# Mask as eight extra contraction rows of the scores, scales moved to the queries, a negated maximum, and an earlier copy of finished values

## The reference

```python
# differential attention, 8 heads x 2 halves of 64
q = rope(q.reshape(B, S, H, 2, d), positions) * (d ** -0.5)
k = rope(k.reshape(B, S, H, 2, d), positions)
allowed = k_chunk[None, :] <= q_chunk[:, None]
s = jnp.where(allowed[None, None, None], einsum('bqhcd,bkhcd->bhcqk', qb, k), -jnp.inf)
p = jax.nn.softmax(s, axis=-1)
a = p[:, :, 0] - lam * p[:, :, 1]
# latent attention, 8 heads, 64 + 32 rows of contraction
sc = (einsum('bqhd,bkhd->bhqk', qn, k_nope) + einsum('bqhd,bkd->bhqk', qp, k_pe)) * scale   # 96 ** -0.5
sc = jnp.where(key_chunk[None, :] <= q_chunk[:, None], sc, -jnp.inf)
p = jax.nn.softmax(sc, axis=-1)
```

## Time and profile before

| what | us |
|---|---|
| median of 3 runs | 3967.03 (3963.65 to 3971.49) |
| the profiled execution, its own time | 3965.26 |
| its span, first to last instruction | 3963.4 |
| what lies around the span | 1.9 |
| differential attention, steps | 119 to 632 |
| latent attention, both layers, first scores to last values | 2947.8 to 3119, 3670.3 to 3844 |

### The profile page before, as it was taken

One profiled execution on the slowest core, in us unless ns is written; L12 is line 12 of the kernel. 1 busy time (PEld: TensorE's weight loads), 2 busy tenths in 40 slices (PEclk: granted clock), 3 DMA queues, 4 the chain that ended last, 5 costly groups with the idle time before them and its releaser, 6 DMA issues. The chain is left out here.

```text
span 3963.4 us, 44407 instructions
## 1 busy us (share of the span) xinstructions
PE 3634.3 (92%) x17688; PEld 2817.6 (71%) x17688; DVE 1662.8 (42%) x2161; ACT 1092.5 (28%) x1653; POOL 1142.8 (29%) x672
## 2 busy tenths in 40 slices
PE   6999987999999999999999998599969969996997
PEld 4777765888888888788888887487626758763565
DVE  5566755311121259641111123456536431363553
ACT  2344443101010116421001011215325310442540
POOL 3344512333333336433333332222201122230111
PEclk8999998999999999999999999799979979998898
DMA  3333322111111121211111110221042121203311
GB/s 122 106 124 131 107 85 80 48 48 48 48 48 48 64 74 54 85 46 48 49 48 48 48 48 21 91 94 53 9 133 54 59 96 43 75 22 90 86 60 59
DMA packets 80128, 267.22 MB, mean 67 GB/s; under 512 B 9424, under 2 KB 10608, under 8 KB 79984
## 3 DMA queue, kind: packets, MB, share of 16 engines
q1 hardware_dynamic: 54464, 191.30, 14.7%
q10 hardware_dynamic: 18608, 48.78, 3.6%
q0 software_dynamic: 6912, 25.17, 1.9%
HBM read 214.62 MB, written 46.40 MB: 66 GB/s over the span
## 5 line engine op out<-in xcount | busy, mean ns | idle before, releaser
L694 POOL CAST tk_w_hi<-tk_w_raw 128x1024 fp32r<-128x1024 f32 x160 | 178.1, 1113 | 1199.4 <-PE tk_acc L191 550.8
L191 PE MATMUL tk_acc<-tk_b_hi,tk_w_hi 128*128 128x512 f32 x1280 | 397.6, 392 | 11.4 <-POOL tk_w_lo L696 11.4
L191 PE MATMUL tk_acc<-tk_a_hi,tk_w_hi 128*128 128x512 f32 x1280 | 398.6, 393 | 3.5 <-POOL tk_w_lo L696 2.7
L191 PE MATMUL tk_acc<-tk_b_lo,tk_w_hi 128*128 128x512 f32 x1280 | 398.2, 392 | 0.0
L191 PE MATMUL tk_acc<-tk_b_hi,tk_w_lo 128*128 128x512 f32 x1280 | 398.1, 392 | 0.0
L191 PE MATMUL tk_acc<-tk_a_lo,tk_w_hi 128*128 128x512 f32 x1280 | 397.9, 392 | 0.0
L696 POOL TENSOR_TENSOR tk_w_lo<-tk_w_raw,tk_w_hi 128x1024 fp32r<-128x1024 f32 x160 | 394.1, 2463 | 12.8
L191 PE MATMUL tk_acc<-tk_a_hi,tk_w_lo 128*128 128x512 f32 x1280 | 397.6, 392 | 0.0
L841 ACT ACTIVATE tk_sq<-tk_r 128x1024 f32<-128x1024 f32 x64 | 67.9, 1061 | 1078.8 <-DVE tk_r L961 1078.8
L936 DVE TENSOR_TENSOR xT<-tk_acc,xT 128x1024 f32<-128x1024 f32 x80 | 98.0, 1225 | 614.9 <-PE tk_acc L191 614.9
L191 PEld LDWEIGHTS tk_acc<-tk_b_hi,tk_w_hi 128*128 128x128 f32 x1280 | 241.0, 188 | 65.0 <-POOL tk_w_lo L696 11.8
(11 more groups left out here) (363 smaller groups left out, 6748.6 us busy)
## 6 DMA issues: line engine op xcount, KB each, us to landing
tk_w_raw<-in_w_trunk SPq DMA_DIRECT2D x160, 512.0 KB, 3.2
da_w_mod<-in_ada_w POOLq DMA_DIRECT2D x48, 512.0 KB, 3.7
pj_w_raw<-in_w_in SPq DMA_DIRECT2D x44, 512.0 KB, 3.3
da_w_raw<-in_w_qkv SPq DMA_DIRECT2D x24, 512.0 KB, 3.7
x_dram<-xT ACTq DMA_DIRECT2D x24, 512.0 KB, 5.9
qk_dram<-xT ACTq DMA_DIRECT2D x32, 256.0 KB
ma_w_raw<-in_w_out SPq DMA_DIRECT2D x16, 512.0 KB, 4.1
xT<-x_dram SPq DMA_DIRECT2D x16, 512.0 KB, 7.9
```

The source lines that it names most:

```text
L191: last = pe.matmul(self.acc[:, u, s * HALF:(s + 1) * HALF], w[:, u, k, :], h[:, k, s * HALF:(s + 1) * HALF], start=(k == order[0] and part ...
L694: pool.tensor_copy(pn.hi[:, u, :, :], pn.raw[:, u, :, :]).then_inc(sems[f"w_hi{u}"], 1)
```

## The change

Four edits.

1. In `ma` the mask becomes part of the score matmuls. Rows 96 to 103 of q and k, one for each block of 128 tokens, are cleared by GpSimd (two memsets of 8 x 4096), then VectorE writes, with eight products of the identity, -1e30 into row 96 + b of q for the first 64 columns of block b, and 1 into row 96 + b of k for the last 64 columns of block b. The scores contract over 104 rows; the mask matmul is gone. TensorE waits for the eight products in place of three small memsets.
2. In `ma` and `da` VectorE's maximum is written with its sign turned, and the product with -scale is gone; the exponential has scale 1.
3. So queries carry the scale: in `mp` ScalarE's copy becomes an activation Copy with a scale; in `da` the four rotation products of queries and keys become `scalar_tensor_tensor` with the scale (or 1) as a third factor.
4. In `da` VectorE's `natural(t - 1)` moves from behind the maxima and rotations to the head of step t. The mask matmul of `da` stays.

```diff
@@ mla_project, ScalarE
-                        act.copy(ab[:, 0, at, :] if at < 2 else o[:, at % 2, :], acc[:, at % 2, :])\
-                            .then_inc(sems["out"], 1)
+                        act.activation(ab[:, 0, at, :] if at < 2 else o[:, at % 2, :], acc[:, at % 2, :], ACT.Copy,
+                                       scale=96 ** -0.5 if order[at] < 6 else 1.0).then_inc(sems["out"], 1)
@@ mixed_back
-        units, kd, scale = 4, 96, 96 ** -0.5
+        units, kd, rows, scale = 4, 96, 96 + SB, 96 ** -0.5
-                    pool.memset(mask[:, :, :], 0.0).then_inc(sems["mask"], 1)
-                    pool.wait_ge(sems["mask"], 1)
-                    pool.memset(mask[:, 0, 0:64], 1.0).then_inc(sems["mask"], 1)
-                    pool.memset(mask[:, 1, 64:128], NEG).then_inc(sems["mask"], 1)
+                    for x in (q, k):
+                        pool.memset(x[kd:rows, :, :, :], 0.0).then_inc(sems["clear"], 1)
-                    pe.wait_ge(sems["mask"], 3)
+                    pe.wait_ge(sems["mask"], 8)
-                            pe.matmul(dst[:, part, :], q[0:kd, u % 2, m, b * P:(b + 1) * P],
-                                      k[0:kd, u % 2, m, part * w:(part + 1) * w], start=True, stop=True)
-
-                        pe.matmul(dst[:, parts - 1, w - P:w], mask[:, 0, :], mask[:, 1, :], start=False,
-                                  stop=True, skip_group_check=True).then_inc(sems["scores"], 1)
+                            last = pe.matmul(dst[:, part, :], q[0:rows, u % 2, m, b * P:(b + 1) * P],
+                                             k[0:rows, u % 2, m, part * w:(part + 1) * w], start=True, stop=True)
+                        last.then_inc(sems["scores"], 1)
-                        dve.tensor_reduce(st[:, t % 4, 0, m:m + 1], score(m, parts, w), axis=AXXY, op=ALU.max)\
-                            .then_inc(sems["max"], 1)
-                        dve.wait_ge(sems["max"], i + 1)
-                        dve.tensor_scalar(st[:, t % 4, 1, m:m + 1], st[:, t % 4, 0, m:m + 1], -scale, None, ALU.mult)\
-                            .then_inc(sems["neg"], 1)
+                        dve.tensor_reduce(st[:, t % 4, 1, m:m + 1], score(m, parts, w), axis=AXXY, op=ALU.max,
+                                          negate=True).then_inc(sems["neg"], 1)
+                    for x, first, value in ((q, 0, NEG), (k, 64, 1.0)):
+                        dve.wait_ge(sems["clear"], 1 if x is q else 2)
+                        for u in range(2):
+                            for m in range(2):
+                                dst = x[kd:rows, u, m, :].rearrange("p (b n) -> p b n", b=SB)[:, :, first:first + 64]
+                                eye = self.ident[kd:rows, kd:rows].rearrange("p (b n) -> p b n", n=1)
+                                dve.tensor_scalar(dst, eye.broadcast_to([SB, SB, 64]), value, None, ALU.mult)\
+                                    .then_inc(sems["mask"], 1)
@@ attention_layer, VectorE (the maximum changes as above)
-                            dve.tensor_tensor(t4[:, 0, :], x, cos, ALU.mult)
+                            dve.scalar_tensor_tensor(t4[:, 0, :], x, by, cos, ALU.mult, ALU.mult)
...
                     for t in range(-1, nb + 4):
+                        natural(t - 1)
                         maximum(t + 1, 0)
                         maximum(t + 1, 1)
                         hp, due = pieces(t) if t >= 0 else (0, [])
                         for p in due:
                             rope(hp, p)
-                        natural(t - 1)
                         combine(t + 1)
```

More of the change, by code:

```diff
@@ L1756, in mixed_back @@
         names = PANEL_SEMS + [
-            "landed0", "landed1", "scores", "max", "neg", "exp", "prob", "pt", "pts", "pv", "out", "link", "mask",
+            "landed0", "landed1", "scores", "neg", "exp", "prob", "pt", "pts", "pv", "out", "link", "clear", "mask",
             "z_in0", "z_in1", "gated", "o_hi", "o_lo", "s_hi", "s_lo", "x_sq", "acc"] + [f"x_ld{n}" for n in range(DK)]
@@ L1768, in mixed_back @@
             st = sb("st", [P, 4, 4, 2])
-            mask = sb("mask", [1, 2, P], BF16)
             sc = ps("sc", [P, 2, S])
@@ L2043, in attention_layer @@
             "w_landed0", "w_landed1", "w_hi0", "w_hi1", "w_split0", "w_split1", "fa", "fb", "fv", "xa", "xb", "v_taken", "rot",
-            "stored", "table", "loaded", "dot", "lam", "landed0", "landed1", "scores", "neg", "max", "exp", "prob", "pt", "pts",
+            "stored", "table", "loaded", "dot", "lam", "landed0", "landed1", "scores", "neg", "exp", "prob", "pt", "pts",
             "pv", "nat", "ot", "out", "o_st0", "o_st1", "o_ld", "link", "mask", "nat_sq", "nat_sum", "nat_root", "nat_normed",
@@ L2382, in maximum @@
                         dve.wait_ge(sems["scores"], 2 * t + m + 1)
[L2383 to L2387 removed]
+                        dve.tensor_reduce(st[:, t % 4, 1, m:m + 1], sc[:, m, 0:parts, 0:w], axis=AXXY, op=ALU.max,
+                                          negate=True).then_inc(sems["neg"], 1)
                     def combine(t):
```

16 lines of the change are left out of this document (6 added, 10 removed).

## The result

In its first comparison the changed kernel took 3922.14 us (median of 4 runs, 3919.32 to 3925.07) and the kernel before 3969.26 (3963.65 to 3971.75): a ratio of 0.9885, 95% interval 0.9873 to 0.9897. A later comparison gave 0.9891 (0.9874 to 0.9908), 3927.49 against 3967.67. The forecast was 3941 us with a range from 3924 to 3957. The direction was right, the size was not: 45 us between the two profiled spans (3963.4 and 3918.5), where the sum said 25.8.

A forecast was written before the change was run, and what follows sets the result against it. TensorE was taken to bound `ma`, while in `da` it waits mostly for VectorE. 19.0 - 4.8 + 7.5 + 4.5 - 0.4 = 25.8 us off the profiled 3965.3, with 1.8 us added for the median: 3941 us, range 3924 to 3957.

The forecast's parts named there:

- Mask matmuls, 19.0 us: In `ma`, removing each mask matmul frees 0.25 us of TensorE in 38 of 64 halves: 9.5 us a layer.
- 26 of 64: Halves of an `ma` layer where TensorE already waits for ScalarE's copy, so removing the mask was to gain nothing.
- about +1 us: In `ma`, added gain from dearer masks at half clock at a layer's head and from the chained last steps.
- Rival (c): More comes back: a third of `da`'s low-clock stretches rise to 2.4 GHz, 4 us, waits 5 more; 3932 us, chance 0.2.
- Preparation, -4.8 us: At the head of each `ma` layer, the mask's memsets and products finish late, by 1.8 and 3.0 us.
- the held case: VectorE's first four mask products are held until GpSimd's second memset ends; mask ready at 12 us.
- nothing lost: Favourable bound for preparing the mask before `ma`'s first scores: no time lost; the other bound was 25.5 us in all.
- 104 rows at no cost: In `ma`, scores contracting over 104 rows in place of 96 keep the same pace by column, priced at nothing.
- Negated maximum, 4.5 us in `da`, nothing in `ma`: VectorE's shorter chain and earlier probabilities give 4.5 us in `da`, between 0 and 8; TensorE's queue hides it in `ma`.
- Moved copy, 7.5 us: In `da`, of 20.0 us of TensorE waits for VectorE's copy, 7.5 return as `prob` or exponentials take over; bounds 2 and 20.
- Scales, -0.4: ScalarE's scaled activation takes 0.1 us more than a copy, ten a layer; 0.2 us a layer shows.

The follow-up runs named there:

- w1_mask_steps_0_1: Changed kernel with the one-row mask matmul put back in the first two steps of each latent layer only; 3934.52 us, ratio 0.9911.
- w3_changed_again: The changed kernel run once more, unaltered, as the control of its batch; 3927.49 us, ratio 0.9891.
- y1_mask_first_unit: Changed kernel with the one-row mask matmul put back in the first of four units of each latent layer only; 3939.98 us, ratio 0.9929.
- y3_no_mask: Kernel before without mask matmuls in `ma` and without mask rows in their place, scores over 96 rows; 3940.31 us, ratio 0.9929.

## Why the prediction was wrong in size

- **Mask matmuls, 19.0 us: over-counted, in the right place.** At 2.4 GHz a unit gained 1.65 us, 6.7 a layer, 13.4 in all. The 0.25 us holds where transposes follow and is 0.16 where values do, and more halves than 26 of 64 run into ScalarE's copies: ten halves at 0.25 us would have been 2.5 us a unit. The steps of 4, 2 and 1 column blocks behind a longer one did not change at all (5.70, 4.40 and 3.12 us in both kernels), as the forecast said; those of 8, 7, 6 and 5 became 0.35 to 0.41 us shorter, that of 3 by 0.16.
- **The clock at the head of `ma`: the term that was missing, about 16 us.** The sum had "about +1 us" for half clock and last steps, and that is the step that failed. It took the length of the low stretch as given and priced only the masks within it. What the runs show is that the mask products at the head lengthen that stretch: without those of the first two steps the rise to 2.4 GHz came 8 us earlier (`w1_mask_steps_0_1` against `w3_changed_again`), though by 1 us only against one layer of `y1_mask_first_unit`. The 16 us are what the 29.4 of the latent layers leave beyond 13.4; 15 of them lie in the two first units, one in the last values of layer 1, which had run at 1.2 GHz before. Rival (c) had the mechanism, with the 28 us at 1.2 GHz of `ma` named in it, and then credited `da` alone. In `da` with filling work the granted clock went only from 0.97 to 0.98.
- **Preparation, -4.8 us: the held case was right, its sizes were not.** One product was held through the second memset (3.70 us), as the earlier trace rows suggested. The Trainium skill ("SBUF — State Buffer", who interferes with whom) has the rule, and the trace after agrees, with 3.70 us in place of 0.41, for a GpSimd operation that only writes. But a memset took 3.5 us, not 4.2, and the products came 0.34 us apart, not 0.45: ready at 9.6 us, not at 12. Loss 0.65 us, nearly the bound "nothing lost".
- **104 rows at no cost: right** (`y3_no_mask`).
- **Negated maximum, 4.5 us in `da`, nothing in `ma`: right in place, too small.** Alone it was worth 9.5 us (5.5 to 13.5); a slot shrinks by 0.19 us, not 0.07, which is likely the reason. On top of the copy it was worth less, some 3 us by the profiles of `da` (495.7 to 493.2). "In `ma` TensorE's queue hides this" holds: later units 38.9 us in both.
- **Moved copy, 7.5 us: right.** 6 to 8 on top by the times, 9.5 alone. That both terms together, 12.0 us, meet the 12.4 and 13.5 measured in `da` is partly luck: each edit alone gave more than its term, and together they share some 5 us, which the sum didn't price as such. With filling work the probabilities took over, as priced; without it ScalarE's copies did, not the exponentials.
- **Scales, -0.4: not seen.** The activation took 1024 ns in the mean of 16, against 1012 for the copy, not the 0.1 us more of the forecast.

From 25.8: -5.6 for the masks, +16 for the clock, +4.1 for the preparation, +1.5 for `da`, +0.4 for the scales make 42 of the 45 us; the other 3 lie in stages that the change does not touch, as differences between two single profiles.

## What to carry to other kernels

A small operation at the head of a stage that starts at the low clock can be worth more than its queue time: ask what it does to the moment of the rise, and look at the units of a loop apart, since the first showed 8 and 10 us where the others showed 1.7. Look at more than one layer or profile too, since over the same matmuls the clock rose after 7.8 us once and after 14.7 another time. When a tiny matmul stands in the queue for a quarter of a microsecond, look at its weight load before removing it; in `ma` widening its tile from one row to 128 gave 21 of the 30 us that removing it gave, while in `da` the same edit showed 3 us at most in the steps. And an edit that clears a wait should be priced together with the edit that shortens what comes next: here the two shared the wait for the probabilities.

## What was not expected of the hardware

- The load of a weight tile of one row did not start until the score before it was over (0.76 us idle), that of a tile of 128 rows did (0.24); 0.25 against 0.06 us of TensorE's queue for the same product in front of transposes. The values' first load, 128 rows by 64 columns, stood idle for 0.76 us as well.
- With four such products in the first two steps TensorE was at 1.2 GHz for 14.9 instead of 6.7 us of the first 24 (for 7.7 in one layer of another kernel with the same start), while after a pause longer by 6.7 us it was for 4.7.
- VectorE's maxima back to back overlap by 0.08 us (2.36 us for two of 1.22).
- A memset of 4096 elements over 8 rows took 3.5 us on GpSimd, and a VectorE product of 0.41 us that began beside it took 3.70.
